# Differential attention: where the value product of every second turn stands among scores and sums of squares

## The reference, cut to what matters

```python
qkv = x @ w_qkv
q, k, v = split(qkv, 3)
q = rms_norm(q.reshape(B, S, 8, 2, 64), q_g) * 64 ** -0.5
k = rms_norm(k.reshape(B, S, 8, 2, 64), k_g)
# per block of 128 queries, per head:
logits = einsum('bhcqd,bhckd->bhcqk', q, k) + bias      # causal
probs = softmax(logits)
w = probs[:, :, 0] - lam * probs[:, :, 1]
o = rms_norm(einsum('bhqk,bhkd->bhqd', w, v), sub_g) * (1 - lambda_init)
```

## Time and profile before

| | |
|---|---|
| runs | 2567.32, 2567.75, 2568.52 us; median 2567.75 |
| the profiled execution | 2567.28 us |
| its span in the profile | 2565.5 us |
| PE busy | 2470.2 us, 96% of the span |
| DVE, ACT, POOL busy | 1341.2, 1042.0, 1147.9 us |
| mean granted PE clock | 0.991 of 2.4 GHz |

### The profile page before, as it was taken

One profiled execution on the slowest core, in us unless ns is written; L12 is line 12 of the kernel. 1 busy time (PEld: TensorE's weight loads), 2 busy tenths in 40 slices (PEclk: granted clock), 3 DMA queues, 4 the chain that ended last, 5 costly groups with the idle time before them and its releaser, 6 DMA issues.

```text
span 2565.5 us, 30689 instructions
## 1 busy us (share of the span) xinstructions
PE 2470.2 (96%) x11318; PEld 1946.6 (76%) x11318; DVE 1341.2 (52%) x1904; ACT 1042.0 (41%) x1387; POOL 1147.9 (45%) x570
## 2 busy tenths in 40 slices
PE   7989999999999999999999998999998998999997
PEld 4658888887676788888876876788887756788886
DVE  6965645544355556356337655551554365552453
ACT  5564322235556642222434253532434343542333
POOL 5844444444343444544443423544445212544443
PEclk9999999999999999999999999999999999999999
DMA  5215545533222255465243312223323122224322
GB/s 147 67 57 164 186 150 181 181 94 110 83 58 74 61 177 181 146 192 168 87 128 99 99 50 74 83 78 111 98 74 98 60 68 66 72 78 121 94 77 67
DMA packets 397552, 273.38 MB, mean 107 GB/s; under 512 B 10067, under 2 KB 379731, under 8 KB 397436
## 3 DMA queue, kind: packets, MB, share of 16 engines
q1 hardware_dynamic: 383612, 221.52, 30.3%
q10 hardware_dynamic: 13824, 50.34, 5.3%
HBM read 269.70 MB, written 2.12 MB: 106 GB/s over the span
## 4 chain that ended last, share of the span: by engine, by line
PE 81%; ACT 6%; DVE 5%; POOL 5%; issue 3%; SPq 0%; DMA 0%; ACTq 0%; DVEq 0%; POOLq 0%
PE ps L688 25%; PE ps L690 25%; PE ps L689 25%; POOL act L2216 2%; POOL weight_lo L2178 2%; DVE act L1776 1%; ACT weight_hi L2314 1%; PE ps L1287 1%; PE ps L928 1%; PE ps L902 1%; PE ps L890 1%; ACT arena L2583 1%; PE ps L887 1%; DVE tmp L1604 0%; PE ps L1227 0%
## 5 line engine op out<-in xcount | busy, mean ns | idle before, releaser
L2178 POOL TENSOR_TENSOR weight_lo<-weight_raw,weight_hi 128x1024 fp32r<-128x1024 f32 (+4 forms) x434 | 996.1, 2315 | 1250.2 <-ACT weight_hi L2314 1248.2
L688 PE MATMUL ps<-u_hi,weight_hi 128*128 128x512 f32 x2312 | 915.4, 396 | 40.8 <-DVE u_lo L1395 29.4
L690 PE MATMUL ps<-u_hi,weight_lo 128*128 128x512 f32 x2328 | 909.9, 391 | 0.0
L689 PE MATMUL ps<-u_lo,weight_hi 128*128 128x512 f32 x2312 | 903.7, 391 | 0.0
L2314 ACT ACTIVATE weight_hi<-weight_raw 128x2048 fp32r<-128x2048 f32 (+2 forms) x223 | 381.2, 1710 | 609.7 <-PE ps L690 575.8
L688 PEld LDWEIGHTS ps<-u_hi,weight_hi 128*128 128x128 f32 x2312 | 436.5, 189 | 158.2 <-DVE u_lo L1395 35.4
L690 PEld LDWEIGHTS ps<-u_hi,weight_lo 128*128 128x128 f32 x2328 | 439.4, 189 | 92.5
L689 PEld LDWEIGHTS ps<-u_lo,weight_hi 128*128 128x128 f32 x2312 | 436.8, 189 | 92.5 <-issue 3.3
L688 PE MATMUL ps<-act_hi,weight_hi 128*128 128x512 f32 x704 | 274.3, 390 | 2.6 <-DVE act_lo L1361 2.6
L689 PE MATMUL ps<-act_lo,weight_hi 128*128 128x512 f32 x704 | 273.9, 389 | 0.0
L690 PE MATMUL ps<-act_hi,weight_lo 128*128 128x512 f32 x704 | 273.9, 389 | 0.0
(11 more groups left out here) (318 smaller groups left out, 2502.9 us busy)
## 6 DMA issues: line engine op xcount, KB each, us to landing
weight_raw<-in_ffn_w_up SPq DMA_DIRECT2D x132, 512.0 KB, 5.2
arena<-in_ada_w ACTq DMA_DIRECT2D x96, 512.0 KB, 5.8
weight_raw<-in_ffn_w_down SPq DMA_DIRECT2D x64, 704.0 KB, 4.6
weight_raw<-in_ffn_w_gate SPq DMA_DIRECT2D x44, 512.0 KB, 3.9
weight_raw<-in_ev_w_in SPq DMA_DIRECT2D x10, 1024.0 KB, 5.3
weight_raw<-in_conv_w_pw SPq DMA_DIRECT2D x16, 512.0 KB, 5.5
weight_raw<-in_ple_w_gate SPq DMA_DIRECT2D x16, 512.0 KB, 3.8
weight_raw<-in_attn_w_qkv SPq DMA_DIRECT2D x16, 512.0 KB, 5.1
```

The source lines that it names most:

```text
L688: pe.matmul(bank, w[0], x[0], start=start, stop=False)
L689: pe.matmul(bank, w[0], x[1], start=False, stop=False)
L690: return pe.matmul(bank, w[1], x[0], start=False, stop=stop)
L2178: low_part = pool.tensor_tensor(w_lo[r][:, cols], raw[r][:, cols], w_hi(k0 + j)[:, cols].bitcast(F32), ALU.subtract)
```

## The change

On PE, in turns 2, 4 and 6, the value unit no longer stands right behind the `qk` unit; it comes after all scores of the turn and before `head_sums`. On DVE, `values_out` of these turns moves behind `reciprocals`. Turn 8 stays as it was. The programs of ACT, POOL and SP are unchanged.

```diff
@@ PE @@
                 for i in range(G + 3):
-                    for name in head_units(i):
-                        unit(name)
+                    units = head_units(i)
+                    if units:
+                        unit(units[0])
                     if i == 1:
...
                     if 0 <= i - 1 < G:
                         score_pairs(i - 1, (2, 3))
+                    if len(units) == 2:
+                        unit(units[1])
                     if i < G:
                         head_sums(i)
@@ DVE @@
-                    if i in (2, 4, 6, 8):
+                    if i == 8:
                         values_out(i // 2 - 1)
                     if 0 <= i - 2 < G:
                         turned_out(i - 2, 0)
...
                     if 0 <= i - 1 < G:
                         logits(i - 1, (2, 3))
                         reciprocals(i - 1)
+                    if i in (2, 4, 6):
+                        values_out(i // 2 - 1)
                     if i == G + 1:
                         finish(G - 3)
```

## The result

The changed kernel takes **2579.26 us** (median of 5 runs, 2578.95 to 2579.49), against 2567.32 us for the kernel before (5 runs): a ratio of 1.0044, 95% interval 1.0032 to 1.0056. That is slower by 11.9 us, outside the range that was given. The profiled execution took 2579.14 us, its span 2577.3.

The account below looks back on a forecast made before the run. PE, busy 96% of the span, was taken as the bound. Turns 4 and 6 (+2.46), turn 2 (-0.4) and odd turns (-1.35) summed to +0.7 us, giving a median of 2568.4 us; range 2565.2 to 2572.3 us.

Parts of the forecast that it names:

- T: On PE, the end of the qk unit of a turn, from which the prediction counted its times; 735.43 in turn 4.
- Odd turns: Turns 3, 5 and 7: second transposes start at T + 2.62 instead of T + 3.08, -0.45 us each, -1.35 in all.
- the late copy: Turns 4 and 6: ACT's copy holds the second transposes until T + 4.31, so the sums start 1.03 us later.
- the wait of `weigh`: Turns 4 and 6: `weigh` needs the values out of PSUM, which the value unit now finishes late; 0.2 us more.
- the short low stretch that I assumed: Turn 2: the clock falls after some 2.4 us idle, costing some 1.1 us; the turn still gives -0.4 us.
- +0.7 us: The forecast's sum over turns 2 to 7: +2.46 for turns 4 and 6, -0.4 for turn 2, -1.35 for odd turns.
- the part on turns 4 and 6: PE's order after the change there: a 0.69 us wait goes, a larger one comes; 1.23 us each, +2.46 us.
- Rival and bounds: Price of a clock fall: up to 1.5 us each in turns 4 and 6; ends of 0 and 1.5 in turn 2.
- The POOL rival: Even turns: POOL's low part holds DVE's logits, +7.6 us in all, 2576.0 us; chance 0.06.
- the full gain: Rival: idling of even turns vanishes because ACT's copy is in time; -7.9 us, 2560.5 us; chance 0.05.
- the clock rival: Rival: the clock falls in turns 4 and 6 too, up to 1.5 us each; +3.7 us, 2571.4 us; chance 0.13.

Follow-up runs that it names:

- a_fill7: The changed kernel plus seven unused matmuls on PE ahead of the second transposes of turns 2, 4 and 6: 2572.03 us.
- a_split_behind: The changed kernel with ACT's first split of turns 2, 4 and 6 moved behind the exponentials of the first four scores: 2568.71 us.
- b_shift36: The kernel before with 36 more matmuls ahead of the value unit of turn 8: 2576.48 us.
- b_shift44: The kernel before with 44 more matmuls ahead of the value unit of turn 8: 2577.96 us in its one run.
- a_turn2: The kernel before with the value unit moved in turn 2 alone: 2570.70 us.
- v_between: The kernel before with the value unit of turns 2, 4 and 6 between the first four scores and the second transposes: 2567.61 us.
- a_turns46: The kernel before with the value unit moved in turns 4 and 6 alone: 2578.31 us in its one run.
- v_halves: The changed kernel with the value unit's first tile between the first four scores and second transposes, the second left in place: 2569.62 us.

## Why the prediction was wrong

**What held.** The waits came out as worked out. Second transposes of turns 4 and 6: T + 4.31 predicted, T + 4.30 measured. Odd turns: T + 2.62 predicted, and 775.85 - 773.29 = T + 2.56 in turn 5, before. `weigh` waits 0.15 us instead of 0.2, the first transposes of turn 2 wait 2.4 us for the mix as said, and in the other turns the mix is never late. `a_fill7` shows the late copy alone at +1.15 us a turn (34.31 against 33.16), where I had 1.23 with the wait of `weigh`. The odd turns gained 1.3 us in all, where I had 1.35. In `a_fill7`, whose clock stays up there, turns 3 to 7 come to +1.0 us together, against +1.1 predicted. Turn 2 with the short low stretch that I assumed was not measured in this order, so that +0.7 us would have stood is not shown.

**The step that failed** is in the part on turns 4 and 6: the clock was taken as 1.00 there, and its fall was a rival with a chance of 0.13. I compared some 1.7 us of idling (1.58 measured) with the 1.5 us idle of the earlier trace rows, which left the clock alone. That row has dense matmuls of 512 columns on both sides; here transposes and scores stand around the gap, and another gap of 0.4 us. I had written that scores and transposes are light work and gave it too little weight; that this is the difference is my reading, and no run separates it. `a_split_behind` and `a_fill7` show that the gap decides in turns 4 and 6: shorten it to 0.4 us or fill it, and the clock stays. A closer case stood in the trace of the kernel before, the second attention, where 1.67, 0.54 and 0.41 us among small matmuls left the clock at 1.00. It too would have pointed to no fall, and the same waits lowered the clock in other kernels: the waits alone did not settle the question, and a chance of 0.13 was too low.

**The term that was mis-sized** is the price of a fall. Rival and bounds took 1.5 us, from the one stretch of 3.4 us in turn 2 of the kernel before. Measured: some 3 us each in turns 4 and 6, with some 7 us at low clock. Turn 2, where I did let the clock fall, had 10 us of it: 2.0 us slower instead of 0.4 faster, a miss of 2.4 us. The rival as priced gave 2571.4; with the measured prices the attention alone gives +8.8.

**Three slips in the arithmetic** did not matter. The POOL rival and the full gain were added to the forecast of 2568.4 us, which already holds the +0.7; from 2567.75 they give 2575.4 and 2559.9 us. The upper end of the range, with the clock rival and 0.5 us for scatter, comes to 2571.9, not 2572.3.

**What was not in the sum at all** is the second attention, 2.9 us, and 0.7 us of a longer low stretch near 1607 us. I assumed that code which the change doesn't touch keeps its clock. `b_shift36` and `b_shift44` show that it may not: a pure delay of 8.2 us costs 1.4 us more there, one of 10.0 us nothing, in one profiled execution of each.

**The other rivals.** POOL did not hold DVE. The third and fourth logits of turn 4, of 128x256, took 0.41 and 0.42 us beside its low part, as ever. The timeline of DVE:

```profile
737.96 0.41 DVE L1709 CUSTOM_DVE_ANT_0 act<-ps,arena 128x256 f32<-128x256 f32 x1
...
738.61 0.42 DVE L1709 CUSTOM_DVE_ANT_0 act<-ps,arena 128x256 f32<-128x256 f32 x1 [0.23 <-PE ps L1002]
```

POOL beside it:

```profile
737.88 4.66 POOL L2183 TENSOR_TENSOR weight_lo<-weight_raw,weight_hi 128x1024 fp32r<-128x1024 f32 x2 [5.79 <-ACT weight_hi L2319]
```

The Trainium skill (SBUF — State Buffer, section "SBUF: two separate sides") lets only VectorE instructions with two SBUF inputs, or in a two-port mode, wait for GpSimd. The trace agrees, and also the other way: the two norm multiplications of turn 4, with two SBUF operands, took 1.42 us in the changed kernel, where POOL had finished, instead of 2.94 in the kernel before, in turn 4 as in turn 5. The full gain did not come either: ACT's split stood where it stands.

## What to carry to other kernels

Moving a block of dense matmuls away from a wait exposes the wait and leaves light work around it, and then the clock is part of the price: here it cost 3 us behind a wait of 1.6 us, about twice the idle time. Before such a move, look on each engine for what the block had covered (here one split of 1.9 us on ACT), and move a part of the block, or that work, with it. When times differ after a change, read the granted clock along the whole span, not only where the code changed: a border case far behind can tip with a mere delay. In turns 2, 4 and 6 a few matmuls in the idle time kept the clock up.

## What was unexpected in the hardware

A wait of 1.58 us on PE, 0.40 us of another just before, amid transposes and scores, was followed by a clock of 0.50 for 3.4 us once and some 7 us in the other cases, and for 10 us behind the 2.4 us of turn 2 (the changed kernel, `a_turn2`, `a_split_behind`); in the kernel before, 3.13 us idle directly in front of dense matmuls had been followed by 3.4 us at low clock. Two waits of 0.4 us were followed by none. In the second attention the same waits of 1.67, 0.54 and some 0.4 us were followed by no low clock in the kernel before, `a_split_behind`, `v_between` and `b_shift44`, by 3.4 us of it in `a_turn2`, `a_fill7` and `b_shift36`, and by 6.8 us in the changed kernel, `a_turns46` and `v_halves`. Whether the length follows from the light work that then runs at the low clock, or from the moment at which the idling falls, was not separated.
